# Gated MLP of a decoder layer on one core: the up-projection as seven block products on groups of 1024 tokens, the down-projection as a phase of its own behind DRAM

## The reference, cut to what matters

```python
D_MODEL, SEQ, D_FF, FFN_CONV = 1024, 2048, 2816, 3
...
def conv_ffn(hn, w_up, conv_w, conv_b, w_down):
    u = causal_dwconv(hn @ w_up, conv_w, conv_b)      # w_up: 1024 x 5632, three taps over tokens
    gate, val = jnp.split(u, 2, axis=-1)
    return (jax.nn.silu(gate) * val) @ w_down         # w_down: 2816 x 1024
...
    h = h + conv_ffn(rmsnorm(h, ffn_norm), w_up, conv_w, conv_b, w_down)
    out = rmsnorm(h, final_norm)
```

## Time and profile before

| what | value |
|---|---|
| median of 3 runs | 3578.9 us (3572.47 to 3580.93) |
| profiled execution | 3568.92 us, its span 3566.8 us |
| mean granted TensorE clock in it | 0.962 |
| first and last matmul of the MLP | 2049.61 us, 3553.76 us |

### The profile page before, as it was taken

The page is one execution under the profiler, slowest core; times in us unless marked ns, Lnnn a source line. Parts: engine busy times, 40 slices in busy tenths (PEclk is TensorE's granted clock), DMA queues, the critical chain, the costliest instruction groups (busy, mean ns, idle before and its releaser), DMA issues. The chain is left out here.

```text
span 3566.8 us, 55094 instructions
## 1 busy us (share of the span) xinstructions
PE 3250.0 (91%) x21296; PEld 2636.3 (74%) x21296; DVE 2018.1 (57%) x3083; ACT 1302.1 (37%) x1945; POOL 492.7 (14%) x650
## 2 busy tenths in 40 slices
PE   5998989589998589889999699999999999999998
PEld 4766767488887368767888588787887788778876
DVE  4656575577757477344444367626772577347752
ACT  3635444455551222112323234314432344234422
POOL 2323233367750011000000000000000000000000
PEclk9999999799999789999999899999999999999999
DMA  3252524512210144330111222333232423242222
GB/s 128 74 177 71 182 76 154 172 56 74 74 48 8 66 158 155 134 136 30 65 65 59 95 94 94 106 107 131 93 111 89 149 94 116 79 150 96 94 100 89
DMA packets 163546, 360.97 MB, mean 101 GB/s; under 512 B 11056, under 2 KB 95280, under 8 KB 151344
## 3 DMA queue, kind: packets, MB, share of 16 engines
q1 hardware_dynamic: 163376, 358.53, 29.8%
HBM read 287.18 MB, written 71.30 MB: 101 GB/s over the span
## 5 line engine op out<-in xcount | busy, mean ns | idle before, releaser
L2495 PE MATMUL ffn_ps<-ffn_hn_high,w_ring_high 128*128 128x512 f32 x1408 | 557.5, 396 | 32.5 <-DVE w_ring_low L2594 28.9
L2495 PE MATMUL ffn_ps<-ffn_hn_low,w_ring_high 128*128 128x512 f32 x1408 | 556.6, 395 | 0.1
L2495 PE MATMUL ffn_ps<-ffn_hn_high,w_ring_low 128*128 128x512 f32 x1408 | 556.6, 395 | 0.0
L2594 DVE TENSOR_TENSOR w_ring_low<-w_ring_raw,w_ring_high 128x2048 fp32r<-128x2048 f32 (+1 forms) x176 | 309.5, 1759 | 354.8 <-ACT w_ring_high L2528 344.3
L2528 ACT ACTIVATE w_ring_high<-w_ring_raw 128x2048 fp32r<-128x2048 f32 (+1 forms) x176 | 261.1, 1484 | 376.7 <-PE ffn_ps L2510 326.0
L2495 PEld LDWEIGHTS ffn_ps<-ffn_hn_high,w_ring_high 128*128 128x128 f32 x1408 | 265.7, 189 | 97.9 <-issue 35.5
L410 PE MATMUL proj<-hn_high,w_high 128*128 128x512 f32 x672 | 281.3, 419 | 36.0 <-POOL w_low L330 36.0
L2495 PEld LDWEIGHTS ffn_ps<-ffn_hn_high,w_ring_low 128*128 128x128 f32 x1408 | 265.6, 189 | 62.8 <-issue 0.3
L2495 PEld LDWEIGHTS ffn_ps<-ffn_hn_low,w_ring_high 128*128 128x128 f32 x1408 | 265.8, 189 | 62.3
L2510 PE MATMUL ffn_ps<-w_ring_high,hidden_high 128*128 128x512 f32 x704 | 280.2, 398 | 12.3 <-DVE w_ring_low L2594 6.9
L2510 PE MATMUL ffn_ps<-w_ring_low,hidden_high 128*128 128x512 f32 x704 | 279.0, 396 | 0.0
(11 more groups left out here) (447 smaller groups left out, 6117.2 us busy)
## 6 DMA issues: line engine op xcount, KB each, us to landing
w_ring_raw<-in_w_up SPq DMA_DIRECT2D x88, 1024.0 KB, 4.8
w_ring_raw<-in_w_down SPq DMA_DIRECT2D x88, 512.0 KB, 3.5
w_ring<-in_w_feat SPq DMA_DIRECT2D x84, 512.0 KB, 3.5
feats<-scratch_scan SPq DMA_DIRECT2D x16, 896.0 KB, 4.5
x_t<-in_x SPq DMA_DIRECT2D x4, 2048.0 KB, 8.0
m_x<-in_x SPq DMA_DIRECT2D x16, 512.0 KB, 3.5
scratch_h<-m_x SPq DMA_DIRECT2D x16, 512.0 KB, 3.1
xa_ring<-in_wkv SPq DMA_DIRECT2D x16, 512.0 KB, 3.5
```

Source lines behind the costliest of these rows:

```text
L2495: mm = pe.matmul(ps[:, 2 * u + g], w[a][:, u, g * D_MODEL + k * P:g * D_MODEL + (k + 1) * P], hn[b][:, k], start=k == a == b == 0, stop=k ...
L2594: dve.tensor_tensor(dst, loads[:, u, 0:n], high_part, ALU.subtract).then_inc(split.sem, 1)
```

## The change

The stage now has two phases with no loop on the device.

**Up phase.** Tokens are taken in two groups of 1024 (`GT`). For a group and a feature tile f the product is a 2 x 2 block product: rows are gate and value of the tile, the depth is cut in two halves of 512, and the tokens in two halves of 512. Strassen's scheme in its form with 15 sums gives the four blocks from seven products `p1` to `p7` of depth 512 (4 pieces by 3 passes, 12 matmuls of 128x512 each). There are 2 x 22 = 44 sets (`SETS`) of seven products, in the order p5, p6, p4, p3, p1, p7, p2. For every set VectorE makes four sums of weights (s1 to s4) and seven sums of results (u2, u4, c12, u3, c22, c21, c11; one operand in PSUM), and seven weight pieces of 128x512 are rounded by ScalarE and split by VectorE. Four sums of tokens (t1 to t4) and seven splits of token pieces, all 128x2048, are made once for a group. There is one buffer for each of the seven weight pieces and token pieces. PSUM's eight banks go round over the products. The gate rows are convolved and put through Silu in the up phase (ScalarE takes the first tap with the bias and a copy of p1), on 128x1024, and stored to DRAM (`gates`); the value rows are stored as they are (`values`).

**Down phase.** For block b and tile f, a step n (88 in all, `DOWNS`), SyncE loads gate, value with two columns ahead, and `w_down` into one of four ring slots, in three transfers; ScalarE takes the value's first tap, VectorE two more and the product with the gate; ScalarE rounds product and weights in one instruction of 128x1536, VectorE splits them in another, and TensorE runs the same 24 matmuls. The parts lie in two buffers (those of token pieces p5 and p6, free by then). The end of a block (add, norm, scaling) is spread over the first steps of the next.

The names below are those of the program: `multiplied` is counted by TensorE at the end of a product, `w_high`/`w_split` and `t_high`/`t_split` by ScalarE and VectorE for a piece's two parts, `down_split` for a step's.

```diff
-                def up(f, i, u, more):
-                    pe.wait_ge(*split.at(p, UP + f))
-                    pe.wait_ge(*up_out.at(p, f - 2))
-                    for g in range(2):
-                        if g:
-                            pe.wait_ge(*added.at(p, back=1))
-                        for k in range(KT):
-                            for a, b in PASSES:
-                                mm = pe.matmul(ps[:, 2 * u + g], w[a][:, u, g * D_MODEL + k * P:g * D_MODEL + (k + 1) * P],
-                                               hn[b][:, k], start=k == a == b == 0, stop=k == KT - 1 and a == 1)
-                        mm.then_inc(up_done.sem, 1)
...
+            LAST_READ = {"p5": "c22", "p6": "u2", "p4": "c21", "p3": "c12", "p1": "p1", "p7": "u3", "p2": "c11"}
+            for s in range(SETS):
+                for i, name in enumerate(PRODUCTS):
+                    n = len(PRODUCTS) * s + i - NPS
+                    if n >= 0:
+                        before, other = divmod(n, len(PRODUCTS))
+                        pe.wait_ge(summed_up[LAST_READ[PRODUCTS[other]]], before + 1)
+                    pe.wait_ge(w_split[name], s + 1)
+                    pe.wait_ge(t_split[name], s // FF_T + 1)
+                    for k in range(HK):
+                        for a, b in PASSES:
+                            mm = pe.matmul(bank(name, s), w_part(name, a)[:, k * P:(k + 1) * P],
+                                           t_part(name, b)[:, k * TB:(k + 1) * TB], start=k == a == b == 0,
+                                           stop=k == HK - 1 and a == 1)
+                    mm.then_inc(multiplied[name], 1)
+            for n in range(DOWNS):
+                b, f = divmod(n, FF_T)
+                pe.wait_ge(down_split, n + 1)
+                for t in range(CB):
+                    if n == 0:
+                        pe.wait_ge(summed_up[DOWN_AFTER[t]], SETS)
+                    for c in range(2):
+                        if f == 0 and b:
+                            pe.wait_ge(added, 2 * CB * (b - 1) + 2 * t + c + 1)
+                        for x, y in PASSES:
+                            mm = pe.matmul(ps[:, DOWN_BANKS[2 * t + c]], down_part(n, x)[:, HID + t * TC:HID + (t + 1) * TC],
+                                           down_part(n, y)[:, c * DH:(c + 1) * DH],
+                                           start=f == x == y == 0, stop=f == FF_T - 1 and x == 1)
+                        if f == FF_T - 1:
+                            mm.then_inc(summed, 1)
+                if f < FF_T - 1:
+                    mm.then_inc(down_used, 1)
...
+            def tap_value(n):
+                f = n % FF_T + FF_T
+                wait_loaded(act, ("down", n))
+                if n >= 2:
...
+                               scale=C["col"]("ffn_conv_w2", f)).then_inc(value_tap, 1)
+            def take_down(n):
+                act.wait_ge(hidden_made, n + 1)
+                if n < 2:
+                    act.wait_ge(multiplied[("p5", "p6")[n]], SETS)
+                elif n % FF_T == 1:
+                    act.wait_ge(summed, 2 * CB * (n // FF_T))
+                else:
+                    b, f = divmod(n - 2, FF_T)
+                    act.wait_ge(down_used, b * (FF_T - 1) + f + 1)
+                act.activation(down_part(n, 0), slot(("down", n))[:, 0:VAL], ACT.Copy).then_inc(down_high, 1)
...
+            for s in range(SETS):
+                g, j = divmod(s, FF_T)
+                more, turn = s + 1 < SETS, g + 1 < GROUPS and j == FF_T - 1
+                w_raw_round("p2", s, 0, 1)
+                if s:
+                    tap_gate(s - 1)
+                if more:
+                    w_sum_round("p5", "s1", s + 1)
+                    w_sum_round("p6", "s2", s + 1)
+                    w_raw_round("p4", s + 1, 1, 1)
+                if turn:
+                    t_sum_round("p6", "t2", g + 1)
+                    t_sum_round("p5", "t1", g + 1)
+                if s:
+                    silu(s - 1)
+                if more:
+                    w_sum_round("p3", "s4", s + 1)
+                if turn:
+                    t_raw_round("p3", "b22", g + 1)
+                copy_p1(s)
+                if more:
+                    w_raw_round("p1", s + 1, 0, 0)
+                    if turn:
+                        t_raw_round("p1", "b11", g + 1)
+                    w_sum_round("p7", "s3", s + 1)
+                else:
+                    tap_value(0)
+                    tap_value(1)
+                    take_down(0)
+                if turn:
+                    t3_round(g + 1)
+                    t_sum_round("p4", "t4", g + 1)
+                    t_raw_round("p2", "b21", g + 1)
+            tap_gate(SETS - 1)
...
+            def t2_sum(g):
+                wait_tokens(dve, "b11", g)
+                t_sum("t2", "p6", tokens("b12", g), tokens("b11", g), g, ALU.add)
...
+            def sum_u2(s):
+                dve.wait_ge(summed_up["p1"], s + 1)
+                dve.tensor_tensor(u2[:], bank("p6", s), rows(s % 2, 0)[:, 2:2 + TB], ALU.add).then_inc(summed_up["u2"], 1)
...
+            def sum_u3(s):
+                dve.wait_ge(multiplied["p7"], s + 1)
+                dve.tensor_tensor(u3[:], bank("p7", s), u2[:], ALU.add).then_inc(summed_up["u3"], 1)
+            def sum_c22(s):
+                dve.wait_ge(summed_up["u3"], s + 1)
+                if s >= 2:
+                    dve.wait_ge(value_stored[s % 2], 16 * (s // 2))
+                dve.tensor_tensor(rows(s % 2, 1)[:, 2 + TB:], bank("p5", s), u3[:], ALU.add).then_inc(summed_up["c22"], 1)
...
+            def hidden(n):
...
+            def low_down(n):
+                dve.wait_ge(down_high, n + 1)
+                dve.tensor_tensor(down_part(n, 1), slot(("down", n))[:, 0:VAL], down_part(n, 0), ALU.subtract)\
+                   .then_inc(down_split, 1)
...
+            for s in range(SETS):
+                g, j = divmod(s, FF_T)
+                more, turn = s + 1 < SETS, g + 1 < GROUPS and j == FF_T - 1
+                if s:
+                    sum_c11(s - 1)
+                w_raw_low("p2", s, 0, 1)
+                w_sum_low("p7", s)
...
+                    gate_tails(s - 1)
+                if more:
+                    s1_sum(s + 1)
...
+                if more:
+                    s2_sum(s + 1)
+                    w_sum_low("p5", s + 1)
+                if s:
+                    gate_tap_two(s - 1)
+                zeros(s)
+                if more:
+                    w_raw_low("p4", s + 1, 1, 1)
+                if turn:
+                    t2_sum(g + 1)
+                    t1_sum(g + 1)
+                if more:
+                    s4_sum(s + 1)
+                    w_sum_low("p6", s + 1)
+                else:
+                    hidden(0)
+                sum_u2(s)
+                if more:
+                    w_sum_low("p3", s + 1)
+                sum_u4(s)
+                if more:
+                    w_raw_low("p1", s + 1, 0, 0)
+                sum_c12(s)
+                if turn:
+                    t_sum_low("p5", g + 1)
+                    t_raw_low("p3", "b22", g + 1)
+                if not more:
+                    low_down(0)
+                sum_u3(s)
+                if more:
+                    s3_sum(s + 1)
+                sum_c22(s)
+                sum_c21(s)
+                if s == LAST - 2:
+                    t3_sum(1)
+                if turn:
+                    t_raw_low("p1", "b11", g + 1)
+                    t_low("p7", g + 1, tokens("b12", g + 1))
+                    t4_sum(g + 1)
+                    t_sum_low("p6", g + 1)
+                    t_sum_low("p4", g + 1)
...
+            def add(b, t, c):
+                dve.wait_ge(summed, 2 * CB * b + 2 * t + c + 1)
+                h = residual(b)[:, t, c * DH:(c + 1) * DH]
+                dve.tensor_tensor(h, h, ps[:, DOWN_BANKS[2 * t + c]], ALU.add).then_inc(added, 1)
...
+            for n in range(DOWNS):
+                b, f = divmod(n, FF_T)
+                if b and f == 1:
+                    dve.wait_ge(h2_in[(b - 1) % 2], 16 * ((b - 1) // 2 + 1))
                     for t in range(CB):
...
+                            add(b - 1, t, c)
+                if n:
+                    low_down(n)
+                    if n + 1 < DOWNS:
+                        hidden(n + 1)
+                if b and f == 2:
+                    mean(b - 1, 0, CB)
+                if b and f == 3:
+                    dve.wait_ge(gain_in, 16)
+                    invert(b - 1, 0, CB)
+                if b and 3 <= f < 3 + CB:
+                    scale(b - 1, f - 3)
...
+            def load_down(n):
+                u = load_at["down", n][0]
+                b, f = divmod(n, FF_T)
...
+                sp.dma_start(ring[:, u, HID:VAL], D["gates"][f, :, b * TB:(b + 1) * TB]).then_inc(loaded[u], 16)
+                sp.dma_start(ring[:, u, VAL:SLOT], D["values"][f, :, b * TB:(b + 1) * TB + 2]).then_inc(loaded[u], 16)
```

(1 more changed line is left out.)

644 lines of the change are left out of this document (414 added, 230 removed).

## The result

| | before | after |
|---|---|---|
| median | 3579.6 us (3572.5 to 3580.9, 4 runs) | 3453.3 us (3451.9 to 3453.7, 4 runs) |
| profiled execution, its span | 3568.9, 3566.8 us | 3451.9, 3449.8 us |
| start of the first and the last matmul of the MLP | 2049.6, 3553.8 us | 2054.6, 3437.4 us |

The ratio is 0.965, interval 0.9634 to 0.9667: 126 us faster by the medians, 117.0 by the two spans, where 77.4 were forecast. The other 8.6 come from the step from span to median: the forecast added the 10 us by which the profiled execution of before lay under its median, and here it lies 1.4 us under.

A forecast was written before the change was run, and what follows sets the result against it. TensorE was taken to bound the MLP. Off: 122.9 us of matmuls, 30.1 of old waits, 0.4 of tail; on: 75.7 of new waits, 0.3 at the start. Net 77.4 off 3578.9 gives 3501.5 us; range 3460 to 3548.

The forecast's parts named there:

- The price of a matmul: Whole MLP: a 512-column matmul costs 0.2327 us while TensorE is fed, so the 5808 that stay take 1351.5 us.
- the ring: Down phase: low part, taps, product, ScalarE and hops take 5.94 us a step, 0.355 over TensorE's time; 30.5 us in all.
- The removed matmuls: Up phase: 3696 matmuls instead of 4224, so 528 fall away from TensorE, 122.9 us off.
- the ring is hidden after all: Rival, down phase: pieces put end to end overlap, leaving TensorE's own pace; 39 us less, 3463 us; chance 0.12.
- The entry: Start of the down phase: first step split 2.2 us after TensorE is free, the second 3.9 us late.
- Three block changes: Down phase: eight adds between a product and a low part, 2.9 us not hidden at each change; 8.7 us.
- Start: Sets 0 and 1: set 0 ends 8.7 us late, set 1 waits 0.4, lower clock adds 2; 11.1 us.
- change of tokens: Around set 21: TensorE waits 6.6 and 10.7 us for low parts on VectorE, plus 2 for restarts; 19.3 us.
- Sets hidden: Up phase in steady state: VectorE and ScalarE keep up with TensorE's 19.55 us a set, 1.8 us to spare.
- VectorE bounds the sets: Rival, up phase: VectorE needs 21.1 us a set, 1.5 over, 44 times; 66 us more, 3568 us; chance 0.12.
- The clock falls in the down loop: Rival, down phase: steps at the lower clock take 10.2 us instead of 5.94; all 88 give 3880 us; chance 0.06.
- Late loads in the down loop: Rival, down phase: landing takes over 13 us for the 4.8 seen; gain gone at 6.8 us a step; chance 0.04.

The follow-up runs named there:

- e7: The kernel before with one unused buffer of 128 bytes a partition ahead of the split weight ring; 3540.0 us, ratio 0.9910.
- e8: The changed kernel with small unused buffers between weight pieces, so each product's weight pieces start 0 to 384 bytes past its token pieces, modulo 512; 3464.4 us.
- e3: The changed kernel with the 12 matmuls of product p2 run twice in each of the 44 sets; 3565.4 us.
- e4: The changed kernel with SyncE's last gate store, residual loads and gain load moved behind loads of later down steps; 3440.2 us.
- e5: The changed kernel with a down step's value taps and product made two steps ahead instead of one, with four value buffers; 3441.0 us.
- e9: The changed kernel with the changes of e4 and e5 together, plus ScalarE's and VectorE's lists at the change of tokens reordered; 3424.5 us.
- run 241: Not a follow-up run: "run" is a verb here, and 241 is an interval in ns between matmuls in the kernel before.

## Why the prediction was wrong, point by point

- **The price of a matmul** (0.2327 us, "I take 0.2327 us as the price of a 512-column matmul while TensorE is fed"): the term that was mis-sized most, 35.0 us. It was read rightly from the earlier trace rows, but it was a price of that placement, which the change replaces. That the new operands all start at the same remainder of 256 comes from the buffer sizes; nobody aimed at it, so what placement gave the change, a good 30 of the 126 us, is luck. e7 and e8 show the cause. With 0.2267 in its place, 35.0 us come off, and the ring of 5.94 us exceeds TensorE's step by 0.5 instead of 0.355, which is 12.5 us in 86 steps: 3501.5 - 35.0 + 12.5 = 3479 us, inside the range.
- **The removed matmuls** (122.9 us): right as a mechanism; e3 gives 119.7 in TensorE's time, 112.1 in the median, since some waits get shorter with it. Against before with its padding (e7) the changed kernel is 3453.3 to 3540.0, 87 us faster, near the 77.4 that were forecast; the other 31 to 40 us (by either median of before) are placement, which the change brought by the way.
- **The ring** (5.94 us a step, 30.5 us), the second mis-sized term: it is 5.49 us a step, and 1.6 us of loss outside the block changes. The links were right, their sizes not. Dependent VectorE instructions start 0.78 us apart here, not 0.90 as in the earlier trace rows, and the way to ScalarE and back costs 0.07 beyond both durations (0.72 and 1.53 for 0.69 and 1.49), not 0.30. I had these from code with loops and registers between the instructions; that this makes the difference is argued, not shown. I gave "the ring is hidden after all" 0.12, with 3463 us; that is what happened, for the smaller ring and not for overlap.
- **The entry** (2.2 + 3.9 us): those two came (2.35 and 3.6), a third one, the 11.4 us ahead of step 3, did not stand in the sum. I had followed SyncE's list for slots ("reloaded some 13 us ahead of its use") in the steady loop and not at its first turn, where the store and the residuals stand ahead. e4 shows it.
- **Three block changes** (8.7 us): 14.4. I had priced the adds between a product and its low part, and not TensorE's wait for the first add, 6.3 us in all, nor the slow matmuls behind such waits, 2.8. With slack in the ring 4.5 are left; e5 shows it.
- **Start** (11.1) and **change of tokens** (17.3 + 2): 10.5 and 18.9. That the sums are this near is luck, as two errors cancel in each. At the start three waits make 5.5 us and slow matmuls the rest of 5.0, where I had 9.1 and 2. At the change the two waits came as described, for low parts on VectorE, but are 6.4 and 9.0 us, with 3.5 for slow matmuls, where I had 6.6, 10.7 and 2. e9 confirms what stood in the way.
- **Sets hidden**, **VectorE bounds the sets** (0.12): hidden, 19.04 us apart with TensorE never idle; e3 speaks against that rival too.
- **The clock falls in the down loop** (0.06): a granted clock of 1.00 from 3220 to 3280 us, where the steps are 5.49 us apart and TensorE waits at each of them, the last row of the windows. The Trainium skill, TensorE: Matmul & The Clock Gate, section "A second HAM failure mode: psum-queue depth-cycling", tells of a clock that swings when TensorE pauses often, if only for a moment, between groups of matmuls. This trace doesn't show it: pauses of 0.05 us at most every 24 matmuls left the clock at 1.00.
- **Late loads in the down loop** (0.04): happened once, at the entry, and not in the loop; the median of a step's three transfers lands in 3.8 to 5.4 us.
- **The mean of 396 ns is the price** (0.02): rightly small. The mean went to 392 with the new price.

## What to carry to other kernels

Before a rate from a trace is carried over to changed code, look for the same operation elsewhere in the same trace: here two rates for one shape stood side by side, and the cheaper one was free for the taking, with 128 bytes of padding. Let the stationary and the moving operand of a matmul start at addresses that are equal modulo 256 bytes, or try it: shown here for fp32r matmuls of 128x512 with a weight load each, and for no other kind. Where a ring of dependent steps is about as long as the bound engine's own step, give it one step of slack. Here the slack cost 3.6 us at the entry and gave back 11.6 behind it. And follow each engine's list through the first and the last turn of a loop, not only through the middle.

## What the runs showed of the hardware

- A stream of weight load and 128x512 fp32r matmul at a granted clock of 1.00 has a price of 0.2267 us when both operands' start addresses differ by a multiple of 256 bytes, and 0.2316 to 0.2333 us when they differ by 32, 64, 96, 128 or 384 (e8; 0.2324 and 0.2333 in before). One exception is p5 in e8 (0.2299 at a difference of 0, behind a slow product). The slow stream is not even: in before, intervals run 241, 232, 231, 232, 228, 230 ns over and over, give or take 2, and in one block 229 and 238 in turn; the fast one has 226 and 227 alone. The Trainium skill, TensorE: Matmul & The Clock Gate, section "Part 2: What happens when you issue a matmul", gives TensorE two independent read ports, one for each operand. By that alone the two addresses should not meet; in these runs the pace depends on their difference. By what mechanism, and whether it is the high or the low parts that pay, was not tried.
- A wait ahead of a matmul disturbs the spacing of the next few. In the changed kernel, ahead of down step 49, an interval of 262 ns instead of 227 is followed by 232 and 231 ns, ahead of step 51 one of 253 by 236, 228, 233 and 231, and then 226 and 227 again.
- A wait of 2 to 3 us is followed by matmuls at the lower clock (0.43 us apart) in some cases and not in others. In the down phase of the changed kernel none came behind intervals of 2.11, 2.30 and 2.36 us, seven each behind 2.35 and 3.01, eight behind 3.59; in e4 none behind 2.97 and 3.02, six behind 3.01.
- Dependent VectorE instructions of 512 columns start 0.03 to 0.04 us after the end of the one ahead in code without loops (rows of the ring above: 0.78 us from start to start for one of 0.75), where the looped code of before shows 0.15.
